# Two sequence mixers in float32: the heads' steps at other tiles, the gate tiles last, retention scores in one bank, and POOL for parts that touch SBUF alone

## The reference, cut to what matters

```python
# retention, per head (chunked in the reference, the same sum): decay g = 1 - 2**(-5-h)
q, k = rotate(q), rotate(k) * 128**-0.5          # pairs 2i, 2i+1 turned by an angle of the position
o[i] = sum over j <= i of g**(i-j) * (q[i].k[j]) * v[j]
o = (o - mean(o)) * rsqrt(var(o) + eps) * gn_w
y_ret = silu(rg) * o
# differential attention, per head, two halves of 64
a = softmax(causal(q1.k1 / 8)) - lam * softmax(causal(q2.k2 / 8))   # partial rotary on q and k
o = a @ v
y_diff = o * rsqrt(mean(o*o) + eps) * subln_w * (1 - lambda_init)
h = h + concat(y_ret, y_diff) @ w_out
```

## Time and profile before

| | us |
|---|---|
| median of 3 runs (2320.88 to 2324.24) | 2322.95 |
| the profiled execution | 2321.68 |
| its span, first to last instruction | 2319.8 |

### The profile page before, as it was taken

How to read it: one execution, slowest core, us unless ns; L and a number is a source line. 1 busy time by engine, 2 the same in 40 slices (tenths; PEclk the granted TensorE clock), 3 DMA queues, 4 the chain that set the end, 5 groups by cost and what they waited for, 6 DMA issues and landing times.

```text
span 2319.8 us, 42837 instructions
## 1 busy us (share of the span) xinstructions
PE 2260.1 (97%) x18118; PEld 2220.4 (96%) x18118; DVE 1538.8 (66%) x2650; ACT 1160.6 (50%) x1826; POOL 39.4 (2%) x53
## 2 busy tenths in 40 slices
PE   7999989999999989999999999999999899999999
PEld 7999879999999988999999999999999799999999
DVE  6655866664765776765775687656665677775763
ACT  5444455444544455544554445445444566665542
POOL 0000000100000000000000000000000000000000
PEclk9999999999999999999999999999999999999999
DMA  8545433865555532655555556556555444452653
GB/s 283 172 162 177 146 109 112 260 203 185 174 171 171 175 116 83 198 187 187 171 194 186 164 196 200 182 178 198 188 169 165 133 146 141 146 175 89 203 190 101
DMA packets 423454, 393.65 MB, mean 170 GB/s; under 512 B 14015, under 2 KB 419647, under 8 KB 423264
## 3 DMA queue, kind: packets, MB, share of 16 engines
q1 hardware_dynamic: 412240, 375.56, 50.3%
q0 software_dynamic: 11024, 15.36, 2.1%
HBM read 389.66 MB, written 7.41 MB: 171 GB/s over the span
## 4 chain that ended last, share of the span: by engine, by line
PE 89%; DVE 8%; ACT 2%; issue 1%; DMA 1%; SPq 0%; DVEq 0%; ACTq 0%
PE ps L1263 28%; PE ps L1262 27%; PE ps L1264 27%; DVE t L823 3%; PE ps L1487 1%; PE ps L1533 1%; PE ps L1512 1%; PE ps L1523 0%; PE ps L1514 0%; PE ps L1535 0%; ACT t L658 0%; DVE t L977 0%; DVE t L851 0%; DVE t L984 0%; DVE t L1037 0%
## 5 line engine op out<-in xcount | busy, mean ns | idle before, releaser
L1262 PE MATMUL ps<-t 128*128 128x256 f32 (+1 forms) x5696 | 1637.3, 287 | 17.2 <-DVE t L823 17.0
L1263 PE MATMUL ps<-t 128*128 128x256 f32 (+1 forms) x5696 | 1624.8, 285 | 0.0
L1264 PE MATMUL ps<-t 128*128 128x256 f32 (+1 forms) x5696 | 1620.2, 284 | 0.0
L1262 PEld LDWEIGHTS ps<-t 128*128 128x128 f32 x5696 | 1079.2, 189 | 27.3 <-issue 19.7
L1263 PEld LDWEIGHTS ps<-t 128*128 128x128 f32 x5696 | 1077.4, 189 | 5.7 <-issue 4.6
L1264 PEld LDWEIGHTS ps<-t 128*128 128x128 f32 x5696 | 1078.1, 189 | 0.0
L823 DVE TENSOR_TENSOR t<-t 128x1024 fp32r<-128x1024 f32 (+1 forms) x728 | 861.8, 1196 | 185.2 <-ACT t L563 183.6
L563 ACT ACTIVATE t<-t 128x1024 fp32r<-128x1024 f32 (+1 forms) x728 | 737.6, 1029 | 308.2 <-PE ps L1264 296.4
L638 ACT ACTIVATE t<-t 128x256 fp32r<-128x256 f32 (+1 forms) x176 | 74.5, 423 | 309.8 <-DVE t L949 309.8
L946 DVE TENSOR_TENSOR t<-ps,t 128x256 f32<-128x256 f32 (+1 forms) x176 | 75.6, 429 | 130.6 <-PE ps L1264 130.6
L939 DVE TENSOR_TENSOR t<-ps,t 128x256 f32<-128x256 f32 (+1 forms) x176 | 75.7, 430 | 116.6 <-PE ps L1264 115.7
(11 more groups left out here) (162 smaller groups left out, 991.2 us busy)
## 6 DMA issues: line engine op xcount, KB each, us to landing
t<-ffn_w_in SPq DMA_DIRECT2D x88, 1024.0 KB, 5.1
t<-ffn_w_gate SPq DMA_DIRECT2D x43, 1024.0 KB, 5.2
t<-ffn_w_up SPq DMA_DIRECT2D x43, 1024.0 KB, 5.5
t<-attn_w_qkv SPq DMA_DIRECT2D x72, 512.0 KB, 3.6
t<-ffn_w_down SPq DMA_DIRECT2D x32, 1024.0 KB, 5.4
t<-ffn_w_out SPq DMA_DIRECT2D x32, 1024.0 KB, 5.3
t<-w_in SPq DMA_DIRECT2D x28, 1024.0 KB, 4.9
t<-ffn_w_down SPq DMA_DIRECT2D x16, 768.0 KB, 4.8
```

The lines of the kernel that those rows point to most:

```text
L1262: pe.matmul(o, hi, xhi, start=i == 0, stop=False)
L1263: pe.matmul(o, hi, xlo, start=False, stop=False)
L1264: ins = pe.matmul(o, lo, xhi, start=False, stop=i == r.nk - 1)
```

## The change

1. `MIX_PAIRS` gives the tiles in a new order: rv moves in front, the four gate tiles rg become the last, 24 to 27. `MIX_STEPS` and `OUT_STEPS` hang the steps behind other tiles.
2. Step R2 is gone. R1 writes all three score blocks of a retention head into one bank: 272, 144 and 16 queries wide, for keys 0 to 127, 128 to 255 and 256 to 271 (before: 16, 128 and 128 keys, 272, 256 and 128 queries wide). One DVE operation multiplies them by the decay, whose table has 432 columns instead of 656 per head. The last block uses keys 144 to 271 with zero decay for those already counted.
3. POOL does the last two of a rotation's four operations (the product with the sines and the sum) and the low part of each head's result. DVE waits before a shuffle until POOL has finished with that buffer, two rotations back.
4. The semaphores tm, vk, mixv, hsq, mean, hroot, hms, hn, yh, yl exist once for the differential and once for the retention heads, each with its own count (`of_head`). The waits on bank 7 follow from a list of its users (`LAST_BANK`).
5. ACT copies the transposed v in one operation instead of two; the product of the 16 first keys for differential heads reads a cleared tile `aT0` of which ACT writes 16 rows. The result of a head lies in `yv` (differential) or in the used row of `qk` (retention).

The diff, cut:

```diff
+NDEC = T + T - P + META
...
+MIX_PAIRS = [("dq", 0), ("dk", 0), ("dv", 0), ("rq", 0), ("rk", 0), ("rv", 0), ("dq", 2),
+             ("dk", 2), ("rq", 2), ("dv", 2), ("rk", 2), ("rv", 2), ("rg", 0), ("rg", 2)]
+MIX_TILES = [(kind, i + j) for kind, i in MIX_PAIRS for j in range(2)]
...
 MIX_STEPS = {
+    4: [("D1", 0)], 6: [("D2", 0)], 8: [("D3", 0)], 10: [("D4", 0), ("D1", 1)], 11: [("D2", 1), ("O1", 0)],
+    12: [("O2", 0)], 13: [("D3", 1), ("R1", 0)], 15: [("D4", 1), ("R3", 0), ("D1", 2)],
+    16: [("R4", 0), ("O1", 1)], 17: [("O2", 1)], 18: [("R1", 1), ("D2", 2)], 19: [("D3", 2)], 20: [("R3", 1)],
+    21: [("D4", 2), ("D1", 3)], 22: [("O1", 2), ("D2", 3), ("R4", 1)], 23: [("O2", 2), ("R1", 2)],
+    24: [("D3", 3)], 25: [("R5", 0)], 26: [("D4", 3), ("R3", 2), ("R5", 1)],
+    27: [("O1", 3), ("O2", 3), ("R4", 2), ("R5", 2)]}
...
+OUT_STEPS = {
+    1: [("R1", 3)], 3: [("R3", 3)], 4: [("R4", 3), ("R5", 3)]}
...
+LAST_BANK = [step for k in sorted(MIX_STEPS) for step in MIX_STEPS[k] if step[0] in ("D2", "D3", "O2")]
...
+                def rotate(kind, i, n):
...
+                    w.wait_ge(S["shuf"], 16 * l + n + 1)
+                    pool.tensor_tensor(turned, turned, rotr[:, 2 * q + 1, c0:T], ALU.mult).then_inc(S["spun"], 1)
+                    w.wait_ge(S["spun"], 16 * l + n + 1)
+                    w.wait_ge(S["evac"], T0[s] + MIX_TILES.index((kind, i)) + 1)
+                    pool.tensor_tensor(qk[:, row, c0:T], m1[:, v, 0:T - c0], turned, ALU.add).then_inc(S["qk"], 1)
+
+                def low_y(kind, i, c):
+                    w.wait_ge(*of_head("yh", l, kind, i))
+                    pool.tensor_tensor(y[:, c, 1, cq:T], yv[:, cq:T] if kind == "d" else qk[:, i, cq:T],
+                                       f32(y[:, c, 0, cq:T]), ALU.subtract).then_inc(S["yl_" + kind], 1)
...
                     src = ps[:, plan.bank[t], 0:n]
                     w.wait_ge(S["mm"], plan.summed[t])
+                    if turn.n > 2:
+                        w.wait_ge(S["qk"], 16 * l + turn.n - 2)
+                    dve.stream_shuffle(sh[:, v, 0:n], src, swap8 if q else swap2).then_inc(S["shuf"], 1)
                     dve.tensor_tensor(m1[:, v, 0:n], src, rotr[:, 2 * q, c0:T], ALU.mult).then_inc(S["evac"], 1)
-                    w.wait_ge(S["dve"], shuffled)
-                    dve.tensor_tensor(sh[:, v, 0:n], sh[:, v, 0:n], rotr[:, 2 * q + 1, c0:T], ALU.mult).then_inc(S["dve"], 1)
-                    w.wait_ge(S["dve"], own.up())
-                    dve.tensor_tensor(qk[:, row, c0:T], m1[:, v, 0:n], sh[:, v, 0:n], ALU.add).then_inc(S["qk"], 1)
...
-                        dve.tensor_tensor(lanes[lane][1][:, cq:T], ps[:, other, 0:NQ], dec[:, i, 384 + cq:384 + T],
-                                          ALU.mult).then_inc(S["rdec"], 1)
-                    elif what == "R2":
-                        other = 3 if lane else 7
-                        w.wait_ge(S["rsc"], 2 * (4 * l + i) + 2)
-                        dve.tensor_tensor(lanes[lane][0][:, :], ps[:, other, 0:384], dec[:, i, 0:384], ALU.mult).then_inc(S["rdec"], 1)
+                        dve.tensor_tensor(lanes[lane][0][:, cq:], ps[:, other, cq:NDEC], dec[:, i, cq:], ALU.mult).then_inc(S["rdec"], 1)
...
+                    else:
+                        pe.matmul(o[:, 0:NQ], v[:, 0, :], aT[:, cq:T], start=True, stop=False)
+                        pe.matmul(o[:, P - cq:NQ], v[:, 1, :], aT[:, T:2 * T - P], start=False, stop=False)
+                        pe.matmul(o[:, 2 * P - cq:NQ], v[:, 2, :], aT[:, 2 * T - P:], start=False, stop=True).then_inc(S["mixv_" + kind], 1)
...
+                        pe.matmul(ps[:, other, cq:T], k[:, 0:P], q[:, cq:T], start=True, stop=True)
+                        pe.matmul(ps[:, other, T:2 * T - P], k[:, P:2 * P], q[:, P:T], start=True, stop=True)
+                        pe.matmul(ps[:, other, 2 * T - P:NDEC], k[:, T - P:T], q[:, 2 * P:T], start=True,
                                   stop=True).then_inc(S["rsc"], 1)
```

More of the change, by code:

```diff
@@ L336 @@
     + ["silu", "prod", "ah", "al"]
-    + ["qk", "gate", "dsc", "dmax", "dexp", "dp", "turn", "at", "tm", "vk", "rsc", "rdec", "mixv", "hsq", "mean",
-       "hroot", "hms", "hn", "rgate", "yh", "yl", "zero"]
+    + ["shuf", "spun", "qk", "gate", "dsc", "dmax", "dexp", "dp", "turn", "at", "rsc", "rdec",
+       "rgate", "zero"]
+    + [f"{name}_{kind}" for kind in "dr" for name in ("tm", "vk", "mixv", "hsq", "mean", "hroot", "hms", "hn", "yh", "yl")]
     + ["cv", "cy", "cyh", "cyl"]
@@ L515, in _, with mixer, step @@
                 pool.dma_start(o, A[name]).then_inc(S["const"], 16)
+            def mixer(s):
+                l, cq = mix_of[s], STAGES[s][1]
+                def rotate(kind, i, n):
+                    c0, q = cq if kind in ("dq", "rq") else 0, 1 if kind in ("dq", "dk") else 0
+                    v, row, turned = n % 2, ROW[kind] + i, sh[:, n % 2, 0:T - c0]
+                    w.wait_ge(S["shuf"], 16 * l + n + 1)
[7 more added lines that the diff above has]
+                                       f32(y[:, c, 0, cq:T]), ALU.subtract).then_inc(S["yl_" + kind], 1)
+                def step(what, i):
+                    if what == "O2":
+                        low_y("d", i, 4 + i)
+                    elif what == "R5":
+                        low_y("r", i, i)
+                n = 0
+                for k, (kind, i) in enumerate(MIX_TILES):
+                    if kind in ROW:
+                        rotate(kind, i, n)
+                        n += 1
+                    for what, head in MIX_STEPS.get(k, ()):
+                        step(what, head)
+                for i in range(KC):
+                    for what, head in OUT_STEPS.get(i, ()):
+                        step(what, head)
             def zeros(s):
                 w.wait_ge(S["evac"], T0[s])
-                pool.memset(vk[:, :, 0, :], 0.0).then_inc(S["zero"], 1)
+                pool.memset(aT0[:, :], 0.0).then_inc(S["zero"], 1)
                 pool.memset(tt[:, :], 0.0).then_inc(S["zero"], 1)
@@ L525, in _ @@
             zeros(plan.mixers[0])
+            mixer(plan.mixers[0])
             for n in range(NH):
@@ L530, in _ @@
             zeros(plan.mixers[1])
+            mixer(plan.mixers[1])
             s = STAGES.index((DIL, META, W_FFN2 + 8))
@@ L972, in rotate @@
                     n, q = T - c0, 1 if kind in ("dq", "dk") else 0
-                    v, row = turn.n % 2, ROW[kind] + i
+                    v = turn.n % 2
                     turn.up()
@@ L1378, in mix_values @@
[L1378 to L1385 removed]
+                    aT, v, o, a0 = lanes[lane][0], vk[:, i % 2 if kind == "d" else 2, :, :], ps[:, bank, :], META - cq
@@ new lines, in mean, with last_bank @@
+                def mean(kind, i, lane, bank):
+                    w.wait_ge(*of_head("hsq", l, kind, i))
+                    pe.matmul(ps[:, bank, 0:NQ], MEAN, lanes[lane][1][:, 0:NQ], start=True, stop=True).then_inc(S["mean_" + kind], 1)
+                def last_bank(what, i):
+                    n = LAST_BANK.index((what, i))
+                    before, j = LAST_BANK[n - 1]
+                    if n == 0:
+                        w.wait_ge(S["evac"], T0[s])
+                        w.wait_ge(S["msr"], s + 1)
+                    elif before == "D2":
+                        w.wait_ge(*of_head("vk", l, "d", j))
+                    elif before == "D3":
+                        w.wait_ge(S["at"], 4 * l + j + 1)
+                    else:
+                        w.wait_ge(*of_head("hms", l, "d", j))
```

175 lines of the change are left out of this document (69 added, 106 removed), and 6 rows, old and new, of the table MIX_STEPS.

## The result

The changed kernel takes 2295.02 us (median of 4 runs, 2294.62 to 2296.26) against 2322.14 in the runs of the kernel before that lay beside it: ratio 0.9883, 95% interval 0.9866 to 0.9900, 27.1 us less. Forecast were 24.5 us less, 2298.4, with a range of 2291 to 2309. A second set of runs of the same kernel gave 2294.92, ratio 0.9880 (0.9865 to 0.9895). The profiled execution has a span of 2294.4 us, 25.4 less than that of before.

What follows compares the result with a forecast made beforehand. TensorE, busy 97% of 2319.8 us, was taken as the bound; 9.3 + 5.0 + 2.2 + 2.6 + 2.3 + 3.0 + 4.5 - 1.6 - 0.8 - 2.0 = 24.5 us less than 2322.95 gave 2298.4, range 2291 to 2309.

Steps and rivals of the forecast that it cites:

- One bank, 9.3 us: Retention scores: TensorE's waits for the decay multiply, at all eight heads, go in full, 9.3 us back.
- Fewer columns, 4.5 us: Retention scores and value products: narrower blocks cut each of 16 sets from 0.65 to 0.36 us, 4.5 us used.
- (a): D2(2), which waited for its bank until DVE's L851, now comes later: all 5.0 us in two mixers back.
- (b): R1(2) and D2(0) waited for the v tile made just before; now it is tiles ahead: 2.2 us back.
- (c): D4 waited for L1024 because DVE reached step 8's softmax late; with DVE relieved, 2.6 us back.
- (d): D3's wait for L1037 falls from 3.4 to 1.1 us, D3(3) waiting no more: 2.3 us back.
- The end of the mixer, 1.6 + 0.8 us: Mixer end: new mean wait less R1(3)'s shorter one costs 1.6 us; last projection's wait for POOL's low half, 0.8.
- rival 2: ScalarE late in tiles 24 to 27, two table loads exposed per mixer: 19.4 us less, 2303.5; chance 0.13.
- POOL: Rotations and low halves: 80 operations at 0.77 us each, POOL busy about 60 us, not a bound.
- Who shares a port: DVE and POOL operations with two SBUF inputs, L823 above all, may keep each other out: 2.0 us charged.
- rival 1: DVE and POOL contention takes DVE's gain, first scores wait longer: 18.1 us less, 2304.9; chance 0.25.
- The clock: Half-clock stretches after waits at mixer ends, left in the sum; without them 3.4 us less, 2295.0; chance 0.08.

## Why the prediction was right, point by point

- *One bank, 9.3 us.* Right in the changed kernel: gone in full, and R3 waits for no decay. Alone with its columns and restarts it gives 12.5 us by run, 15.0 by my terms. The profile has one more half-clock stretch (1.7), 0.4 of wait on the decay and the new wait of 1.5 on ScalarE's copy in the difference.
- *Fewer columns, 4.5 us.* Right: 4.2 by the start times. The remainder of the mixers (8.1 us) leaves 3.9 for the restarts, put at 3.0; they were not measured by themselves.
- *The steps at other tiles.* (a) 5.0 back, as measured; that the order is needed for it is shown by the run in the old order, which has the 5.0 again. But it is not the order alone: without POOL the same step waits 3.7 for its v tile. D2(2) stands right behind that tile, with only R1(1) between; "one or more tiles ahead", which I used for R1(2) and D2(0), holds for those and not for it, and I did not look there. (b) 2.2 back. Either part is enough for it: these waits are gone in the old order with POOL and in the new order without it. (c) 2.6 back, and with everything on DVE 3.2 are there: DVE's relief, as I had it. With POOL they are gone in the old order as well. (d) D3 was put at 1.1, measured 1.3; here too either part alone does most of it (1.5 in the old order with POOL, 1.7 in the new one without, 3.5 with neither).
- *The end of the mixer, 1.6 + 0.8 us.* The new wait of the mean was put at 2.2 and is 2.2; R1(3) at 4.0, is 4.7; the low half at 0.8, is 0.8. ScalarE being late in tiles 24 to 27 (rival 2) did not come: the one table load there that PE feels is that in the chain of d3, which stood there before the change as well, and the run with the early load prices what can be taken back of it at 0.8 us in each mixer.
- *POOL.* Its operation of 272 columns was put at 0.77 and takes 0.77 undisturbed. In the changed kernel the sums take 1.57 in the mean, so the 80 operations make 91.5 us where I had about 60.
- *Who shares a port.* Three of my own signs of being wrong came: POOL's sums are over 1.1 us (1.57), the first scores wait on them (2.4), and L823, now L864, grew where they meet (1.82 against 1.22). I charged 2.0 us, a number picked between nothing and full exclusion; the effect that PE feels is the first scores' wait, 2.4 instead of 0.35, so about 2. That the two agree is luck. The mechanism of rival 1 is the one that holds: the lines do exclude each other (0.76 against 1.64, 1.22 against 1.82). Its price was wrong. I took DVE's period as unchanged; it fell from 2.67 to 2.45, since mostly POOL was the one held up (0.87 us more for its sum, 0.60 more for L864). Seven rotations lie ahead of the softmax of step 8, at 7 x 0.22 = 1.5 us. Measured from the mixer's mean, that softmax ends at 31.9 us of the first mixer in the changed kernel and at 33.5 with everything on DVE, 1.6 earlier, which is what D4(0) waits there; and PE, held up at the first scores, comes about 1.0 us later to D4(0) (1.32 of wait there instead of 0.34). That is why (c) came back after all. The rule cited from the Trainium skill, SBUF — State Buffer, Who interferes with whom, agrees with these rows in kind: two SBUF inputs against a POOL instruction that reads SBUF contend. That the second to start blocks fully fits them roughly: L864 lost 0.60 us where 0.74 of POOL's product were left, and POOL's sum lost 0.87 where 1.0 of L864 was left.
- *The clock.* I left both stretches in the sum; one went, 1.7 us. 24.5 + 1.7 = 26.2, against 26.4 in the mixers by the profiles and 27.1 by the medians. Which one goes was not foreseen: the kernel before has its second stretch 0.6 us behind R1(3)'s wait in the second mixer, and the changed kernel has the same wait of 2.3 us there and no stretch.
- *The range.* Its high end is 2304.9 + 5 = 2310, not 2309; nothing hangs on it.

The sum was right, but one view behind it was not: I credited POOL's part with 2.6 us and charged 2.0 for the port and 0.8 for the last low half, nearly nothing. Taken off, it costs 11.8 us: 5.4 more idle by the profiles, since waits come back that the new order alone does not prevent (D2(2) 3.7, D4(0) 3.2, the mean 1.2 more), and half-clock stretches behind them. My expectation for that run (2295 to 2299) failed by the same step.

## What to carry to other kernels

List the waits of the bottleneck with what would be late next if the named one were on time: here a step whose bank was made free waited for its operand instead (5.0 us became 3.7) until a second edit came. Before a gain of a few us is put down to edits helping each other, count the half-clock stretches: of 4.3 us more than apart, only 1.2 show as idle. Moving work between DVE and POOL was worth it here even though they hold each other up, since it is mostly POOL that waits and its result is mostly not wanted soon; making one wait for the other by a semaphore cost 32 us. Where TensorE is 97% busy, the idle it still has is dearer than it looks, since a wait of 1.6 to 2.5 us can be followed by 3.4 us at half clock, 1.7 more.

## What the runs showed of the hardware that I had not expected

- Runs of one kernel differ by whole stretches of 3.4 us at clock 0.50, the 1.2 GHz level, in the mixers and outside: in the run with the early table load 2287.3 and 2292.1 to 2292.7 for the same program. With everything on DVE, in the execution profiled, five of them lay in the mixers, each behind a wait of 1.6 to 2.3 us, but two waits of 1.8 and 1.7 in its first mixer had none; the changed kernel has waits of 1.3 and 1.1 us without one, and in its second mixer also one of 2.3 us without. What else decides is open.
- A POOL product or sum of 128 x 272 float32 takes 0.77 us, the sum up to 1.64 if it starts while DVE is in its 128 x 1024 operation on two SBUF tensors; that operation of DVE takes up to 1.82 instead of 1.22. DVE's operations that read PSUM and one SBUF tensor stay at 0.42 to 0.43 beside POOL.
- A float32 matmul with full weights and 16 columns takes PE 0.14 us from its start to the next, one with 144 columns 0.25: from 144 down to 16 the time falls by 0.11, half of what the 0.17 per 100 columns of the earlier trace rows would make.
